# GpSimd adds the squares behind four norms, TensorE multiplies the sum with ones once or twice

## The reference

```python
def _rmsnorm(x, g):
    xf = x.astype(jnp.float32)
    y = xf * lax.rsqrt(jnp.mean(xf * xf, axis=-1, keepdims=True) + EPS)
    return (y * g.astype(jnp.float32)).astype(x.dtype)

for i in range(DEPTH):                      # first block, DEPTH = 2
    h = rms_norm(x, norm_mix[i])
    x = x + mixer_i(h)
    h = rms_norm(x, norm_ffn[i])
    x = x + conv_ffn(h, ffn_w_gu[i], ffn_conv_w[i], ffn_conv_b[i], ffn_w_down[i])
return rms_norm(x, norm_final)
```

## Time and profile before

| | us |
|---|---|
| median of three timed executions | 1178.5 |
| lowest, highest | 1174.4, 1180.8 |
| the profiled execution | 1174.7 |
| its span in the profile | 1172.9 |
| busy time of TensorE, VectorE, ScalarE, GpSimd | 1109.7, 744.1, 575.6, 443.9 |

### The profile page before, as it was taken

One profiled execution on the slowest core, in us unless ns is written; L12 is line 12 of the kernel. 1 busy time (PEld: TensorE's weight loads), 2 busy tenths in 40 slices (PEclk: granted clock), 3 DMA queues, 4 the chain that ended last, 5 costly groups with the idle time before them and its releaser, 6 DMA issues.

```text
span 1172.9 us, 23510 instructions
## 1 busy us (share of the span) xinstructions
PE 1109.7 (95%) x9169; PEld 1059.6 (90%) x9169; DVE 744.1 (63%) x1071; ACT 575.6 (49%) x831; POOL 443.9 (38%) x421
## 2 busy tenths in 40 slices
PE   7899899999999969999999999998998999999998
PEld 6797689999999848999999999998997988999998
DVE  5577857767555874777656465446656657777543
ACT  4555645455533554544544437735345545555433
POOL 4354422666502641366632112212543014666400
PEclk9899999999999989999999999998999999999999
DMA  9541127666655422666655553252432454666552
GB/s 290 184 142 37 37 74 216 179 179 188 187 181 162 145 72 73 175 183 179 181 187 184 167 172 117 81 159 88 120 133 86 166 144 110 188 188 187 188 170 83
DMA packets 226408, 175.40 MB, mean 150 GB/s; under 512 B 8720, under 2 KB 207632, under 8 KB 226208
## 3 DMA queue, kind: packets, MB, share of 16 engines
q1 hardware_dynamic: 225056, 173.00, 49.4%
q10 hardware_dynamic: 1248, 1.35, 0.4%
q0 software_dynamic: 32, 0.03, 0.0%
HBM read 173.32 MB, written 1.05 MB: 149 GB/s over the span
## 4 chain that ended last, share of the span: by engine, by line
PE 75%; DVE 9%; ACT 7%; issue 4%; POOL 2%; DMA 2%; SPq 0%; DVEq 0%; ACTq 0%; POOLq 0%
PE psum L613 22%; PE psum L619 22%; PE psum L614 22%; DVE w_l L1676 2%; ACT w_h L1252 2%; DMA raw<-in_nsa_w_in 2%; ACT work L1388 2%; PE psum L1110 1%; POOL work L2517 1%; PE psum L641 1%; PE psum L647 1%; DVE work L1861 1%; ACT work L1327 1%; ACT work L1527 1%; POOL work L2519 1%
## 5 line engine op out<-in xcount | busy, mean ns | idle before, releaser
L613 PE MATMUL psum<-xh,w_h 128*128 128x256 f32 (+2 forms) x1792 | 448.3, 287 | 14.7 <-ACT w_h L1309 7.4
L614 PE MATMUL psum<-xl,w_h 128*128 128x256 f32 (+2 forms) x1792 | 442.0, 284 | 0.0
L613 PEld LDWEIGHTS psum<-xh,w_h 128*128 128x128 f32 x1792 | 339.0, 189 | 19.1 <-ACT w_h L1309 7.4
L614 PEld LDWEIGHTS psum<-xl,w_h 128*128 128x128 f32 x1792 | 339.8, 190 | 0.6
L1676 DVE TENSOR_TENSOR w_l<-raw,w_h 128x2048 fp32r<-128x2048 f32 x92 | 204.8, 2226 | 152.1 <-ACT w_h L1252 152.1
L1252 ACT ACTIVATE w_h<-raw 128x2048 fp32r<-128x2048 f32 x92 | 167.4, 1821 | 214.5 <-PE psum L619 201.7
L619 PE MATMUL psum<-xh,w_l 128*128 128x256 f32 (+2 forms) x1792 | 251.4, 283 | 1.2 <-DVE w_l L1676 1.2
L619 PEld LDWEIGHTS psum<-xh,w_l 128*128 128x128 f32 x1792 | 230.3, 189 | 2.1 <-DVE w_l L1676 1.8
L2424 POOL TENSOR_TENSOR work<-work 128x256 f32<-128x256 f32 x66 | 161.6, 2449 | 140.9 <-ACT work L1435 140.9
L2015 DVE TENSOR_TENSOR w_l<-raw,w_h 128x2048 fp32r<-128x2048 f32 x66 | 151.3, 2293 | 12.8 <-ACT w_h L1431 12.1
L613 PE MATMUL psum<-hid_h,w_h 128*128 128x256 f32 (+1 forms) x592 | 146.7, 283 | 1.0 <-DVE work L2306 0.8
(11 more groups left out here) (307 smaller groups left out, 1420.4 us busy)
## 6 DMA issues: line engine op xcount, KB each, us to landing
raw<-in_ffn_w_gu SPq DMA_DIRECT2D x88, 512.0 KB, 4.6
raw<-in_w_in SPq DMA_DIRECT2D x26, 1024.0 KB, 5.2
raw<-in_ffn_w_down SPq DMA_DIRECT2D x40, 512.0 KB, 4.6
raw<-in_w_ffn_up SPq DMA_DIRECT2D x22, 512.0 KB, 4.0
raw<-in_w_ffn_gate SPq DMA_DIRECT2D x22, 512.0 KB, 5.2
raw<-in_w_ffn_down SPq DMA_DIRECT2D x20, 512.0 KB, 4.5
raw<-in_nsa_w_in SPq DMA_DIRECT2D x9, 1024.0 KB, 5.3
raw<-in_swa_w_qkv SPq DMA_DIRECT2D x5, 1024.0 KB, 5.5
```

The source lines that it names most:

```text
L613: mm(dst, parts[0][:, k, cols], high, start=first, stop=False)
L614: mm(dst, parts[0][:, k, cols], low, start=False, stop=False)
```

## The change

- Norms 1 and 3: GpSimd adds the squares of chunks 1 to 6 onto chunk 0's (`add_squares`), each waiting for the addition before. TensorE multiplies that sum and chunk 7's squares (`sum_two`), behind the first chunk of the feed-forward's first slab, where eight multiplications stood between and behind the projection's chunks. ScalarE's squares of chunks 4 to 7 wait for the additions that free their place in `sq` instead of for TensorE.
- Norms 2, 4 and 5: GpSimd adds the squares of chunks 4 to 7, too, and each of its squares and additions waits for the one before. TensorE multiplies once (norm 2) or twice (norms 4 and 5) in `sum_all`: behind the opening at norm 2, behind the opening and chunk 2 at norms 4 and 5. `sum_first` and `sum_rest` are gone. ScalarE's last scaled square waits for the first addition of `sqb`. GpSimd's two copies of constants stand behind its additions.

```diff
         SQ_AT = {0: 0, 1: 8, 2: 16, 3: 20, 4: 28, 6: 32, 7: 40, 8: 48}
-        SS_AT = {0: 0, 1: 8, 2: 16, 3: 21, 4: 29, 6: 39, 7: 47, 8: 55}
+        SS_AT = {0: 0, 1: 8, 2: 10, 3: 11, 4: 13, 6: 15, 7: 23, 8: 31}
+        ADD_AT = {1: 0, 3: 6}
+        def sq_slot(i, c):
+            return c % 4 if i not in ADD_AT or c < 4 else (1, 2, 3, 1)[c - 4]
...
-            def sum_first(l):
...
-            def sum_rest(l):
...
+            def sum_all(l):
+                pe.wait_ge(sq_all, l + 1)
+                mm(bank[7][:, 0:T1], ones, sq[:, 0, 0:T1], start=True, stop=True, skip_group_check=True).then_inc(ss_step, 1)
                 if l == 1:
+                    mm(bank[7][:, T1:2 * T1], ones, sqb[:, 0, 0:T1], start=False, stop=True, skip_group_check=True).then_inc(ss_step, 1)
+            def sum_two(i, T):
+                pe.wait_ge(sq_added, ADD_AT[i] + 6)
+                mm(bank[7][:, 0:T], ones, sq[:, 0, 0:T], start=True, stop=False).then_inc(ss_step, 1)
+                pe.wait_ge(sq_ready, SQ_AT[i] + 8)
+                mm(bank[7][:, 0:T], ones, sq[:, sq_slot(i, 7), 0:T], start=False, stop=True).then_inc(ss_step, 1)
...
+                        if stream is not None and q == 0 and norm - 1 in ADD_AT:
+                            sum_two(norm - 1, T)
...
-            out_proj(11, (at_out, 0), T1, 1, source=(at_h, at_l))
+            out_proj(11, (at_out, 0), T1, None, source=(at_h, at_l))
...
             opening(M_SWA, T1, 0, STREAMS[2])
+            sum_all(0)
...
-            out_proj(M_SWA + 5, (at_out, 8), T1, 3, source=(at_h, at_l))
+            out_proj(M_SWA + 5, (at_out, 8), T1, None, source=(at_h, at_l))
...
-            project2(2, 12)
+            project2(2, 3)
+            sum_all(1)
+            project2(3, 12)
...
-                    if c >= 4:
+                    if c >= 4 and i in ADD_AT:
+                        act.wait_ge(sq_added, ADD_AT[i] + c - 3)
+                    elif c >= 4:
                         act.wait_ge(ss_step, SS_AT[i] + c - 3)
...
-                act.wait_ge(ss_step, SS_AT[i] + 8)
+                act.wait_ge(ss_step, SS_AT[i] + (2 if i in ADD_AT else 8))
...
+                    if i in ADD_AT:
+                        add_squares(i, T, max(c - 1, 1), c + 1, t0)
+            def add_squares(i, T, c0, c1, t0=0):
+                for c in range(c0, c1):
+                    pool.wait_ge(sq_ready, SQ_AT[i] + c + 1)
+                    line.put(G.tensor_tensor(sq[:, 0, t0:T], sq[:, 0, t0:T], sq[:, sq_slot(i, c), t0:T], ALU.add), sq_added)
+                    line.settle()
...
-                pool.wait_ge(ss_step, SS_AT[4 if l else 2] + 1)
                 for c in range(4, 8):
                     pool.wait_ge(proj_taken, N_FFN[l] + 44 + c + 1)
-                    line.put(G.tensor_tensor(sq[:, c % 4, 0:T1], xT[:, c, 0:T1], xT[:, c, 0:T1], ALU.mult), sq_rest)
+                    line.put(G.tensor_tensor(sq[:, 1, 0:T1], xT[:, c, 0:T1], xT[:, c, 0:T1], ALU.mult))
+                    line.settle()
+                    line.put(G.tensor_tensor(sq[:, 0, 0:T1], sq[:, 0, 0:T1], sq[:, 1, 0:T1], ALU.add), sq_all if c == 7 and not l else None)
+                    line.settle()
+                    if l:
+                        pool.wait_ge(sqb_rest, c - 3)
+                        line.put(G.tensor_tensor(sqb[:, 0, 0:T1], sqb[:, 0, 0:T1], sqb[:, (1, 2, 3, 1)[c - 4], 0:T1], ALU.add),
+                                 sq_all if c == 7 else sqb_added)
+                        line.settle()
```

33 lines of the change are left out of this document (9 added, 24 removed).

## The result

The changed kernel takes 1181.2 us in the median of 20 runs (1178.8 to 1187.6), the kernel before 1176.5 in the median of its 20 beside them. One of these 20 took 2157.1 us; the ratio leaves it out and goes by means, and the median of the other 19 is 1175.2. The ratio is 1.0042, with a 95% interval of 1.0028 to 1.0055: 3.3 to 6.5 us slower, 4.9 in the middle. The prediction said +3.6 and 1182.1. In what follows "before" and "after" are the two kernels, and their row names in the table, `e1` and so on, are the experiments'. The profiled execution took 1183.4 us (span 1181.6) at a mean granted clock of 0.979, against 0.988 before.

The account below looks back on a forecast made before the run. The chain of waits is three quarters TensorE; removed matmuls gain only where others wait for it. -1.35 - 0.44 + 2.8 - 1.3 - 0.9 + 4.8 = +3.6 us on 1178.5 gives 1182.1 us; range 1174.5 to 1187.5.

Parts of the forecast that it names:

- What a multiplication with ones costs, and the down projections: Each holds TensorE 0.44 us; one removed in the first layer's down projections, two in the second's, gain 0.44 and 0.88 us.
- First output projection: First attention's output projection: VectorE paces two chunks at 6.13 us, feed-forward starts at 182.0; gain 1.35 us.
- GpSimd's additions cost nothing: First attention's output projection: six additions fit between GpSimd's copies, costing nothing unless each takes over 1.3 us.
- Second output projection: Second attention's output projection: same pattern as the first, feed-forward starts at 470.2; gain 1.3 us.
- the 3.24 us gap: Gap ahead of 808.23, followed by half clock from 809.4 to 816.0; nearest row for a fall at the second block's input.
- First opening: Second attention's projections: eight chained GpSimd operations ahead of the root end at 382.4, reciprocal starts at 383.75; loss 2.8 us.
- Second block's input: Twelve GpSimd operations end at 675.1, TensorE stands 3.8 us; loss 2.3 us, or 4.8 with a clock fall, which was taken.
- The fall: Second block's input: clock drops to half at 675.8 for 6.6 us, making the loss 4.8 us instead of 2.3.
- A: Rival: clock stays up in the 3.8 us gap at the second block's input; +1.1 us, 1179.6; chance 0.26.
- B: Rival: GpSimd's additions are hidden at 0.61 us an operation in both openings; -6.4 us, 1172.1; chance 0.09.
- C: Rival: clock falls in the opening of the second attention's projections too; +8.8 us, 1187.3; chance 0.14.
- D: Rival: output projections give nothing, GpSimd's additions late beside VectorE's low parts; +2.7 us on the forecast, 1184.8; chance 0.09.

Follow-up runs that it names:

- e1: Kernel before with only the two output projections' norms (1 and 3) as in the change; openings and down projections untouched: median 1179.0 us, ratio 1.0019.
- e5: Changed kernel, but ScalarE makes the last four chunks' plain squares in both openings and GpSimd only adds: median 1175.4 us, ratio 0.9987 against before.
- e6: Changed kernel with 10 small unused bf16 matmuls in TensorE's wait ahead of the second feed-forward: 1181.4 us, ratio 1.0058 against before.

## Why the prediction was right

The change is slower, by so little that two timings could not tell it, as the forecast had it, and the time lay 0.9 us from it. That closeness is partly luck. The forecast started from 1178.5 us, 2.0 above the median of the 20 runs beside the changed kernel, and its change of +3.6 was 1.3 below the measured 4.9. Inside the +3.6 errors cancelled too: against the stages of the profiled execution the projections were too good by 0.5 and 1.7 us, the two openings too bad by 0.65 and 1.1.

- **What a multiplication with ones costs, and the down projections.** 0.44 and 0.88 us were predicted, 0.43 and 0.97 measured. Right, and in six of the eight profiles for each: 0.39 to 0.45 and 0.95 to 1.00. `e5` and `e6` gain only 0.20 and 0.19 in the first layer, and two kernels 0.71 and 0.72 in the second.
- **First output projection.** The additions of the odd chunks come 6.05 us apart (predicted 6.13; VectorE's timeline below), and the feed-forward starts at 181.74, 0.26 earlier than said. The step that failed is "GpSimd's additions cost nothing". It asked only whether they end in time, which they do, and not what they do to VectorE's low parts, which took 0.9 us each instead of half of that. The row that said so was there: the prediction itself used VectorE and GpSimd holding each other up for the openings, and forgot it here. Gain 0.85 instead of 1.35.

```profile
173.96 0.42 DVE L1968 TENSOR_TENSOR xT<-psum,xT 128x256 f32<-128x256 f32 x1
...
180.01 0.42 DVE L1968 TENSOR_TENSOR xT<-psum,xT 128x256 f32<-128x256 f32 x1
...
186.05 0.42 DVE L1968 TENSOR_TENSOR xT<-psum,xT 128x256 f32<-128x256 f32 x1
```

- **Second output projection.** The feed-forward starts at 472.20 - 1.94 = 470.26 with the wait filled, where 470.2 was predicted. Gain 0.58 and not 1.3, mostly because VectorE's low parts are held here too: the first chunk takes 474.80 - 472.20 = 2.60 us to its low terms, where 1.99 are needed. Then the term that no case had: the clock falls behind a wait of 1.99 us and takes 0.9 or more back, so the stage loses 0.34 to 0.41, in `e5` 0.87. The prediction took the 3.24 us gap as the nearest row, and looked for falls only behind gaps as long as that. This is the largest error, 1.7 us.
- **First opening.** 2.8 predicted, 2.12 to 2.15 measured in the seven kernels and executions with its eight operations. The mechanism was right: the low part of a slab stretches one square to 2.54 us. Two durations were too long: the rest took 0.61 to 0.83 each instead of 0.83 throughout, and the low part cost GpSimd 1.9 us and not 2.3. The reciprocal beside the cast was not stretched (1.75 us), as the forecast had taken it.
- **Second block's input.** 2.3 predicted without a fall, 2.0 measured; 4.8 with one of 6.6 us, and 3.7 and 3.9 measured with one of 6.8. The fall was over-priced, 2.5 us where 1.7 and 1.9 were measured. The prediction put its start 4.45 us behind the start of the gap, when the wait is over; it came 1.6 us behind it, so that 1.5 of its 6.8 us lay in the wait, where TensorE has nothing to lose. And it was shorter or missing in three of five profiles.
- **The rivals.** A (the clock stays up in this gap) is what the openings-only kernel did, whose code at this place is that of after. Both profiles of after had a fall, of 6.8 and of 3.4 us; so A looks like one outcome of the same code, not shown for after itself. B is refuted: TensorE waits 1.6 and 3.1 us for GpSimd, and both waits stand in the path to the root. GpSimd's price for an operation of 256 columns was 0.61 to 0.68 us for a square and 0.72 to 0.83 for an addition, apart from the four of these twenty that VectorE's low parts stretched (1.03 to 2.67). The GPSIMD Engine Reference of the Trainium skill (section 3.1) gives 2.6 cycles an element, 0.55 us as an estimate; the trace nearly agrees for a square (0.61) and not for an addition. C (a fall in the first opening) is in none of the eight profiles that have additions there. D was half right: the additions were in time, but they held VectorE.

**What stays open.** From the stages, the change costs 1.3 us with the clock up, 1.0 for the fall behind the wait ahead of the second feed-forward (mean of five profiles), and at the second input 1.1 us more in the mean of five kernels (0, 0.75, 0.95, 1.7, 1.9). That is 3.4 us. The runs say 4.9, with an interval from 3.3. The rest, if it is one, must be in unchanged code, most likely in its half clocks; that is argued and not shown. Behind the 2.06 us gap of the second attention one came in six of the eleven profiles of kernels with anything changed but the fillings, and in none of the two profiles of before and the one with its gaps filled; but 37 of the 83 timed runs of before look like having them too. Whether the change makes them more frequent, and how, I cannot tell from so few profiles.

## What to carry to other kernels

Matmuls taken from an engine that then waits are paid back twice: by the wait of the engine that took the work (here GpSimd in a chain of 8 and 12 operations ahead of a root), and by TensorE's clock behind the wait. Make the operation itself cheaper before moving it: a multiplication with ones cost 0.11 us with float32r operands instead of 0.44, and needed nobody else. In the timed runs even that showed only with the gaps of unchanged code filled (ratio 0.9944, against 0.9992 without), and what float32r does to the last digits of the sums is not measured here. Compare two kernels by the offset of an instruction that both have, stage by stage: it resolved 0.03 us where the medians of 12 runs resolve 2.

## What the runs showed of the hardware

- A wait of 1.99 us was followed by a half clock of 3.4 us in six of six profiles, one of 1.56 us (first projection) in none of eight, one of 3.15 in four of five, one of 3.24 ahead of the earlier trace rows in all that left it unfilled. With small bf16 matmuls in the wait there was none. The prediction had looked for a fall only where a gap was about as long as the 3.24 us one.
- The length of a wait alone does not tell whether a fall comes. In code that no kernel here changes, a wait of 1.94 us at 102 was followed by one in 6 of 14 profiles, one of 2.01 near 895 in 3, the 2.06 us one of the second attention in 6, and one of only 1.00 us at 152 in 4. And the clock fell with no wait of over 0.3 us in the 7 us before: at 80 to 82 in nine profiles, close behind 32 matmuls of 30 columns, and at 788 to 794 in seven. After at the first of these places, where TensorE is busy throughout:

```profile
82.00:84.00 2.00, 2.00 (x11) 0.50 0.04 12
```

- A half clock cost less than half its length wherever it could be priced: 3.4 us cost 0.9 to 1.45 at the second projection, 6.8 us 1.7 to 1.9 at the second input, 0.3 at the 8.4 us gap and 2.9 at the 3.24 us gap. The cheap ones lay partly inside the wait (1.5, 1.05 and 4.0 us of the 6.8), the dear one wholly behind it.
- VectorE's operations with two inputs in SBUF and GpSimd's hold each other up, in both directions: a square of 0.61 us took 2.54 to 2.67 under a low part, and a low part of xT of about 0.45 took 0.93 beside an addition. VectorE's low part of a slab took 2.82 us instead of 2.29 where an addition of GpSimd's was under way as it began, and 2.29 where GpSimd's square began behind it. VectorE's reciprocal, which has one input, took its 1.75 us though 0.85 of them lay beside a cast of GpSimd's, which took 1.74. The GPSIMD Engine Reference of the Trainium skill (section 1) names VectorE's instructions with two SBUF inputs as those that contend; the trace agrees in all these cases.
